# Three edits of order in a hybrid attention and feed-forward layer: a copy on ScalarE, a sum on VectorE, a scaling given to GpSimd

## What is computed

```
q_mla = apply_rope_tail(rms_norm(q, mla_q_norm_g), cos, sin)
k_mla = apply_rope_tail(rms_norm(k_mla, mla_k_norm_g), cos, sin)
o_mla = causal_block_attention(q_mla, k_mla, v_mla)
```

## Time and profile before

| | |
|---|---|
| median of 3 runs | 1418.54 us (1418.39 to 1419.47) |
| the profiled execution, its own time | 1418.58 us |
| its span in the trace | 1416.9 us |
| TensorE (PE) busy | 99% of the span |
| VectorE (DVE), ScalarE (ACT), GpSimd (POOL) busy | 73%, 49%, 12% |
| granted TensorE clock | 0.9 or more of full speed in all 40 slices, mean 1.0 |

### The profile page before, as it was taken

One profiled execution on the slowest core, in us unless ns is written; L12 is line 12 of the kernel. 1 busy time (PEld: TensorE's weight loads), 2 busy tenths in 40 slices (PEclk: granted clock), 3 DMA queues, 4 the chain that ended last, 5 costly groups with the idle time before them and its releaser, 6 DMA issues.

```text
span 1416.9 us, 18996 instructions
## 1 busy us (share of the span) xinstructions
PE 1407.4 (99%) x6938; PEld 1189.4 (84%) x6938; DVE 1039.1 (73%) x1534; ACT 687.3 (49%) x1117; POOL 167.4 (12%) x174
## 2 busy tenths in 40 slices
PE   9999999999999999999999999999999999999999
PEld 7999888888788888878888888888888888888887
DVE  6797556656876558749736888888877777688886
ACT  6344456656555441256413755455555555534332
POOL 2002611113361021114000100000000000000000
PEclk9999999999999999999999999999999999999999
DMA  7023121241121222357632122222222223990222
GB/s 273 2 74 123 28 70 52 63 146 37 55 61 40 83 75 84 83 208 238 239 110 89 57 85 84 88 90 90 74 90 88 66 85 133 322 386 5 97 75 82
DMA packets 130967, 149.81 MB, mean 106 GB/s; under 512 B 11386, under 2 KB 95789, under 8 KB 130605
## 3 DMA queue, kind: packets, MB, share of 16 engines
q1 hardware_dynamic: 130688, 148.54, 31.8%
q10 hardware_dynamic: 189, 0.08, 0.0%
HBM read 111.70 MB, written 36.31 MB: 104 GB/s over the span
## 4 chain that ended last, share of the span: by engine, by line
PE 97%; DVE 1%; ACT 1%; DMA 0%; issue 0%; SPq 0%; POOL 0%; ACTq 0%
PE ps L2547 29%; PE ps L937 18%; PE ps L2856 5%; PE ps L2857 5%; PE ps L2858 5%; PE ps L2947 4%; PE ps L1144 3%; PE ps L3509 2%; PE ps L3510 2%; PE ps L3511 2%; PE ps L1121 2%; PE ps L432 2%; PE ps L434 2%; PE ps L433 2%; PE ps L1841 2%; PE ps L473 2%
## 5 line engine op out<-in xcount | busy, mean ns | idle before, releaser
L2547 PE MATMUL ps<-split_arena 128*128 128x512 f32 x1320 | 306.4, 389 | 0.8 <-ACT up_part L2432 0.8
L2547 PEld LDWEIGHTS ps<-split_arena 128*128 128x128 f32 x1320 | 247.7, 188 | 52.5 <-issue 1.2
L937 PE MATMUL ps<-split_arena 128*128 128x512 f32 x1152 | 290.1, 399 | 0.5 <-ACT plain_arena L972 0.4
L937 PEld LDWEIGHTS ps<-split_arena 128*128 128x128 f32 x1152 | 208.7, 188 | 41.2 <-issue 1.5
L2730 ACT ACTIVATE down_ops<-down_all 128x1024 fp32r<-128x1024 f32 x77 | 81.5, 1062 | 114.6 <-PE ps L2858 112.7
L2749 DVE TENSOR_TENSOR down_ops<-down_all,down_ops 128x1024 fp32r<-128x1024 f32 x77 | 94.2, 1225 | 45.5 <-ACT down_ops L2730 45.4
L2547 PE MATMUL ps<-up_b,split_arena 128*128 128x512 f32 x528 | 127.1, 390 | 0.0
L2858 PE MATMUL ps<-down_ops 128*128 128x512 f32 x308 | 119.9, 389 | 0.0
L2857 PE MATMUL ps<-down_ops 128*128 128x512 f32 x308 | 119.9, 389 | 0.0
L2856 PE MATMUL ps<-down_ops 128*128 128x512 f32 x308 | 119.9, 389 | 0.0
L2547 PEld LDWEIGHTS ps<-up_b,split_arena 128*128 128x128 f32 x528 | 99.0, 188 | 20.4
(11 more groups left out here) (461 smaller groups left out, 2644.3 us busy)
## 6 DMA issues: line engine op xcount, KB each, us to landing
plain_arena<-in_w_in SPq DMA_DIRECT2D x24, 512.0 KB, 3.8
scr_gate<-plain_arena SPq DMA_DIRECT2D x48, 256.0 KB, 2.0
plain_arena<-scr_gate SPq DMA_DIRECT2D x24, 512.0 KB, 4.5
plain_arena<-in_w_up SPq DMA_DIRECT2D x22, 512.0 KB, 5.2
up_raw<-in_w_up SPq DMA_DIRECT2D x22, 512.0 KB, 4.7
scr_act<-plain_arena SPq DMA_DIRECT2D x22, 512.0 KB, 2.7
down_all<-scr_act SPq DMA_DIRECT2D x18, 512.0 KB, 9.6
down_all<-in_w_down SPq DMA_DIRECT2D x18, 512.0 KB, 10.4
```

The source lines that it names most:

```text
L937: mm = nc.tensor.matmul(m.ps[:, self.banks[half], :], w[:, k, :], src[:, k, h * BANK:(h + 1) * BANK], start=(j == 0), stop=(j == self.PER_ ...
L2547: mm = nc.tensor.matmul(o, self.w[j][w][:, k, :], self.h[j][k][h], start=(j in self.OPENS and k == 0 and n == 0), stop=(k == self.HK - 1 a ...
```

## The change

Four things move. In `UpProjection`'s ScalarE order for i=1, `copy_u2(1)` goes from behind split 2 to behind split 4, ahead of copy_c12(0). In both attentions `out_sum` goes from the end of VectorE's step s (s = 5, 9, 13, ...) to step s+1, behind `norm` and the low parts of p, ahead of `maximum`. In mla the two scalings of head 1 go from VectorE to GpSimd, where they stand behind the power and ahead of the wait for `norm(1)` and the gate unit; VectorE keeps the two turnings by position, waiting for `late_rows`. VectorE's wait for `rstd_done` goes from the end of step 0 to ahead of `maximum(2)` in it.

```diff
--- before.py
+++ after.py
@@ -1337,6 +1337,8 @@
             if s:
                 for f in self.fills_of("p", s - 1):
                     self.split_lo(dve, f)
+            if s % 4 == 2 and s > 4:
+                self.out_sum(dve, s // 4 - 1)
             if self.later:
                 self.later(dve, s, True)
             if s + 2 < ATT_STEPS and i != 6:
@@ -1346,8 +1348,6 @@
             if s < ATT_STEPS:
                 for f in self.qk_fills(s):
                     self.split_lo(dve, f)
-            if s % 4 == 1 and s > 4:
-                self.out_sum(dve, s // 4 - 1)
             if s % 4 == 2 and s > 4:
                 self.out_lo(dve, s // 4 - 1)
             if self.later:
@@ -1623,9 +1623,9 @@
         if h == 1:
             pe.wait_ge(rows, 1 + "qk".index(what))
         else:
-            pe.wait_ge(late_rows, 2 * (h - 2) + 1 + "qk".index(what))
-
-    def scale(which, h, half, V=nc.vector, step=m.dve_step):
+            pe.wait_ge(late_rows, 2 * (h - 1) + 1 + "qk".index(what))
+
+    def scale(which, h, half, V=nc.vector, step=m.dve_step, done=None):
         a, g = ((k, gk), (q, gq))[which]
         if half is None:
             x, r = a[:, :, h, :].rearrange("p (f t) d -> p f t d", f=2), rstd[:, :, which, :, h].unsqueeze(3).to_broadcast([P, 2, PAIRS, QK])
@@ -1635,7 +1635,11 @@
             x, r = a[:, tiles, h, :], rstd[:, half, which, :, h].unsqueeze(2).to_broadcast([P, PAIRS, QK])
         step(V.tensor_tensor(x, x, r, ALU.mult))
         x = a[:, tiles, h, NOPE:QK]
-        step(V.tensor_tensor(x, x, g[:, NOPE:QK].unsqueeze(1).to_broadcast([P, x.shape[1], ROPE]), ALU.mult))
+        last = V.tensor_tensor(x, x, g[:, NOPE:QK].unsqueeze(1).to_broadcast([P, x.shape[1], ROPE]), ALU.mult)
+        if done is None:
+            step(last)
+        else:
+            last.then_inc(done, 1)
 
     def rope(which, h, tiles, sn, cs, tmp, V=nc.vector, step=m.dve_step):
         a = (k, q)[which]
@@ -1647,7 +1651,7 @@
         step(V.tensor_tensor(x1, x1, tmp[1], ALU.subtract))
         return V.tensor_tensor(x2, x2, tmp[0], ALU.add)
 
-    LATER = {0: ((1, 1, 0),), 2: ((1, 1, 1), (1, 0, 0)), 4: ((1, 0, 1),)}
+    LATER = {2: 1, 4: 0}
     FIRST_IN_STEP = 4
     MOVED = 5
     moved = [q[:, :, 0, i * ROPE // 2:(i + 1) * ROPE // 2] for i in range(4)]
@@ -1657,20 +1661,19 @@
         for which in (1, 0):
             scale(which, h, None, nc.gpsimd, m.pool_step)
             rope(which, h, slice(0, TT), *moved[0:2], moved[2:4], nc.gpsimd, m.pool_step).then_inc(late_rows, 1)
-            pool.wait_ge(late_rows, 2 * (h - 2) + 2 - which)
+            pool.wait_ge(late_rows, 2 * (h - 1) + 2 - which)
 
     def later(dve, s, first):
         if s == MOVED and not first:
             for i in range(2):
                 nc.vector.tensor_copy(moved[i], kept_rope[:, i]).then_inc(tables_moved, 1)
+        if s == 0 and first:
+            dve.wait_ge(rstd_done, 3)
         if s not in LATER or first != (s == FIRST_IN_STEP):
             return
-        for h, which, turned in LATER[s]:
-            if turned:
-                rope(which, h, slice(0, TT), kept_rope[:, 0], kept_rope[:, 1], [kept_tmp[:, i] for i in range(2)]).then_inc(rows, 1)
-            else:
-                dve.wait_ge(rstd_done, 3)
-                scale(which, h, None)
+        which = LATER[s]
+        dve.wait_ge(late_rows, 2 - which)
+        rope(which, 1, slice(0, TT), kept_rope[:, 0], kept_rope[:, 1], [kept_tmp[:, i] for i in range(2)]).then_inc(rows, 1)
 
     fill = m.gate_fill
     att = Attention(m, "mlaa", QK, lambda h, t: q[:, t, h, :], lambda h, t: k[:, t, h, :],
@@ -1753,12 +1756,13 @@
         pool.wait_ge(prep, 1)
         fill.gpsimd(pool, 1)
         nc.gpsimd.tensor_tensor(by_head[:, :, 1:H], by_head[:, :, 1:H], power[:, :, 1:H], ALU.pow).then_inc(rstd_done, 1)
-        pool.wait_ge(att.normed, 2)
-        fill.gpsimd(pool, 1)
-        m.pool_step.on(pool)
         pool.wait_ge(rstd_done, 3)
         pool.wait_ge(k_out, 3)
         pool.wait_ge(q_out, TT)
+        for which in (1, 0):
+            scale(which, 1, None, nc.gpsimd, m.pool_step, late_rows)
+        pool.wait_ge(att.normed, 2)
+        fill.gpsimd(pool, 1)
         for h in range(2, H):
             later_head(pool, h)
             fill.gpsimd(pool, 1)
@@ -3222,12 +3226,15 @@
                 if i > 1:
                     up.scale_v(act, i - 1)
                 up.split_hi(act, 4, i)
+                if i == 1:
+                    up.copy_u2(act, 1)
                 up.copy_c12(act, i - 1)
                 up.scale_g(act, i - 1)
                 up.split_hi(act, 3, i)
                 if more:
                     up.split_hi(act, 2, i + 1)
-                up.copy_u2(act, i)
+                if i > 1:
+                    up.copy_u2(act, i)
                 if i == 1:
                     up.copy_p7(act, 1)
                 if more:
```

## The result

| | before | after |
|---|---|---|
| median | 1418.81 us (6 runs, 1418.39 to 1419.47) | 1424.29 us (6 runs, 1424.15 to 1424.47) |
| span in the trace | 1416.9 us | 1422.4 us |
| TensorE, VectorE, ScalarE, GpSimd busy | 99%, 73%, 49%, 12% | 99%, 73%, 48%, 12% |

What follows compares the result with a forecast made beforehand. TensorE, busy 99%, was taken to bound the kernel, so only its stands could move the time. Terms -0.99 + 0.3 + 1.7 = +1.0 us on 1418.58 gave 1419.6 us, range 1416.7 to 1421.2.

Steps and rivals of the forecast that it cites:

- Edit 1: Up projection, copy_u2(1) moved ahead: the stand before product 5(1) goes, -0.99 us, bounds 0 and -0.99.
- Edit 2: Both attentions, out_sum moved behind norm: no gain at fox step 18, new stand before p(19), +0.3 us, bounds -0.5 and +0.7.
- Edit 3: Mla, head 1's scaling on GpSimd: step 0's second keys turn +1.8 to +2.4 us late, p(3) wins 0.43; net +1.7.
- A: Mla step 0: VectorE and GpSimd don't exclude each other, scaling is free; 1416.7 to 1417.5 us, chance 0.20.
- B: Mla step 0: VectorE wins the turns, stand 0.3 to 1.0 us, net -0.8 to 0.2; 1417.8 to 1418.8 us, chance 0.17.
- rival C: GpSimd's scaling in mla step 0: exclusion costs more, keys' turn 3.4 us late, net +3.1; 1421.7 us, chance 0.11.

Runs made afterwards that it cites:

- all mended: Kernel before with u2's copy moved, head 1's scaling on GpSimd behind head 0's keys, GpSimd yielding to norm(6) and norm(8), sum unmoved: 1417.86 us against 1418.73.

## Why the prediction was wrong

- **Edit 1.** Right in mechanism, mis-sized: -0.99 forecast, -0.75 measured. The step that failed is "I take the full -0.99 us", which says that no other wait takes part of the place: silu and `copy_p7(2)` on ScalarE take 0.24 us back.
- **Edit 2.** Forecast +0.3 us, measured +2.0. Right: no gain at fox step 18 because GpSimd's gate unit holds `norm(18)`, and the new stand before p(19), 0.40 us for 0.3. Wrong: "Elsewhere the values follow the turn and six or more gate matmuls (1.4 us), which covers the sum." The values were covered, and `out_hi` on ScalarE was not, nor the gate copies behind it. I had named that wait at step 18 only, and priced it on VectorE. The same wait is behind the 0.8 us at the ends of heads 1 and 3 in mla, where I had put 0.
- **Edit 3, step 0.** The alternation came out operation by operation. Forecast: VectorE waits 3.0 to 3.6 us, the keys' turn moves by 1.8 to 2.4, p(3) gives 0.43 back. Measured 3.1, 1.9 and 0.44. The lower of my two figures assumed, without a row for it, that VectorE's operation gets in 0.15 us before GpSimd's record ends; all four did so by 0.14 to 0.15 us. Most of the 0.44 is given back at step 5 (0.30). Rivals A and B fall here. Two slips beside it changed nothing in the forecast: the power had ended at 363.06, before `second("k")` began, so it ran beside `second("q")` alone; and B's upper end of 0.2 does not come out of its own terms, which give -0.1.
- **Edit 3, steps 6 and 8.** The step that failed is "Heads 2 and 3 wait for the tables at 387.00 anyway." It took their start as fixed and harmless. They wait for the tables and so start within 0.1 us of `norm(6)`, and the two exclude each other. The rows of before had shown how near that was: L1298 issued at 386.93 in the trace, L1636 at 387.00 with 1.97 us. I used that 1.97 as an upper price in rival C and didn't ask who had come second and by how much. The three moved waits turned that order, and the late `norm(8)` then met the gate unit. In the changed kernel these collisions cost 0.66 and 1.68 us, 2.3 of its 5.5. They were no rival, so C, which lay on the right side, had the wrong place.
- **The sum.** The change was forecast at +1.0 us and measured at +5.5. Of the 4.5 between them 2.3 are the two collisions, 1.7 the sum's move, 0.3 the turn in step 5 and 0.2 the copy. By the starts: fox 1.2, first keys to p(3) 1.9 - 0.4, step 5 0.3, steps 6 and 8 2.3, the sum in mla 0.8, up -0.8 to -1.0: 5.1 to 5.3 of 5.5. The single edits give -0.75 + 1.96 + 5.43 = +6.6. They don't add up to 5.5, for two reasons that show. `norm(6)` is held as long in both (1.94 us), but it is issued 0.6 us earlier against TensorE's work when the sum isn't ahead of it, so TensorE stands 0.66 us for 1.26. And the lone scaling's profiled execution had a clock drop of 1.25 us that the changed kernel's has not; how much of it lies in the median of five is not measured.
- **Range.** It was built on terms for operations that I had found in the way. It had no term for a lost race between two engines 0.07 us apart. C came out on the slow side for another reason, and its 1421.7 us still lies 2.6 under what was measured.

## What to carry to other kernels

Where two engines exclude each other, look in the trace for pairs of their instructions issued within a tenth of a microsecond: each is a branch that any edit can turn, at the price of the longer instruction, and a wait that orders them is cheap (0.8 us of GpSimd here, felt by no engine in the kernel with all mended). One such branch can bring the next. A moved step is to be followed into the list of every engine that waits for it, down to what is queued behind that wait. A gain that rests on a removed stand is to be looked for again one round of the loop later.

## What the runs showed of the hardware

- The exclusion holds for small strided operations as for large ones: a rope operation of 64 elements per partition, 0.22 us, took 1.40 us beside a GpSimd scaling of 1.54. It holds for `norm` too, which reads one tile and a column: 1.94 us for 0.69. It doesn't hold beside GpSimd's memset, and `second("q")` ran at 0.22 to 0.23 us per operation beside the 4.94 us power, which has SBUF inputs. Why the power is no hindrance stays open.
- Three waits that are long met made 0.09 us on GpSimd, with no exception in the five kernels that have them there and the five that don't, through a wait instruction of 43 ns of its own, and decided over 3 us.
- A stand of TensorE of 1.74 to 1.76 us was followed by about 3 us at half the granted clock in two of three profiled executions, at 1.25 us of time; the six times of the changed kernel lie within 0.3 us of each other, and the profiled one shows no drop behind the same stand. What decides it was not tried.
